# Semaphore clears of the first block's programs moved into the next program, those of the last stages merged

## The chip, the cores and the metric

The kernel runs on one core of a Trainium2 chip. The metric is the device time of one execution in microseconds (us). The engines are PE (TensorE, matmuls; PEld is its weight load), DVE (VectorE), ACT (ScalarE), POOL (GpSimd) and SP (SyncE, which here only issues DMAs). Each engine runs its own instruction stream; the streams meet through semaphores. A small letter q behind an engine's name in a row (PEldq, POOLq) marks an instruction of its sequencer, such as a semaphore clear, a drain or a wait.

## The reference

Two transformer blocks over 256 tokens of width 1024, in float32, one after the other:

```
x = first_block(...)     # modulated norm, then attention + long convolution + Fourier mixing, gated;
                         # then x + g2 * expert_choice_moe(h2, router, w_gate, w_up, w_down), 16 experts
return second_block(x, ...)   # two layers, each: x + 0.5*g1*swiglu(h); three mixers; x + 0.5*g3*swiglu(h)
```

The arithmetic, the tiles and the transfers are the same in both kernels. Only the housekeeping between programs differs, so nothing more of the reference is needed.

## The kernel before

The kernel is a row of hand-written programs. A program is one `nc.Block()`: in it every engine has its own list of instructions, and at its end all five engines meet in a barrier (a drain on each engine, then a semaphore event that POOL collects and gives back). A program belongs to a `Stage` (L268). A stage owns on-chip buffers (`sb`) and semaphores (`sem`), and both are given back when the `with` statement of the stage is left.

The semaphores must be zero again before they are used anew or before the kernel runs again. So `Stage.__exit__` (L298) opens a second `Block` after the program, a clean-up: every fifth semaphore is cleared by POOL (L303), the next by SP (L308), then by PE (L313), ACT (L318) and DVE (L323), all five engines side by side, and then they meet in that block's own barrier. In the profile the clean-up's barrier has line L299. Nothing else runs in a clean-up, and the next program can't start before it is over.

The stages nest. In order of time, with the line that the barrier of the stage's program has in the profile:

- `whole` holds 11 semaphores that show when a feed-forward panel has landed (`ff_here`), and encloses everything.
- `first` (L2771) holds 8 semaphores of the expert panels and encloses the first block. In it:
  - `mixer` (L2778) holds 16 semaphores, and encloses four programs: `front` (its program's barrier is L2606), `project_in` (L650), `attention` (L380) and `project_out` (L975).
  - a stage named `moe` (L2799) with buffers alone and no semaphore, around the program `moe` (L1184).
- `trunk` (L3495) holds 4 semaphores and encloses the second block: `first_layer` (L3525), `between` (L3555) and `last` (L3589).

Every stage with semaphores has one clean-up, so there are 12: after `front`, `project_in`, `attention`, `project_out`, `mixer`, `moe` and `first` in the first block, and after `first_layer`, `between`, `last`, `trunk` and `whole` in the second. Where two stages end together, as `project_out` and `mixer` do, their clean-ups follow each other with nothing between them.

`first_layer` and `between` already clear most of their semaphores inside their own programs: `clear_early` (L288) has POOL clear them (L291) while the other engines finish the layer. These two stages keep this in both kernels.

What sets the order of the work around the clean-ups:

- `project_in` starts with matmuls on panels that `front` loaded (L755).
- `attention` starts with DMAs for the next program's weights (L384) and with score matmuls (L392).
- `project_out` issues the first six expert panels of 2 MB (L1003) as its buffers come free.
- `moe` starts with routing: transposes on PE (L1265), then a chain on DVE. Its SP loads three more panels at once (L1188, L1190), and then one more for each panel that PE has consumed (L1193, waiting for `panel_done`). Its 16 experts have 12 panels each.
- `first_layer` starts with DVE and ACT making the normalized input, then matmuls on panels that landed during `moe` (L1629).
- POOL has no program in `project_in`, `attention`, `project_out`, `moe` and `last`: it only waits in their barriers.

Of the kernel before, what the change touches and what calls it, by code (L numbers as in the profile page):

```python
# [267 lines left out]
class Stage:  # L268


    count = 0

    def __init__(self, nc, name):
        Stage.count += 1
        self.nc, self.name = nc, f"{name}_{Stage.count}"

    def __enter__(self):
        self.stack, self.sems = ExitStack(), []
        return self

    def sb(self, name, shape, dt=F32):
        return self.stack.enter_context(self.nc.sbuf_tensor(f"{self.name}_{name}", shape, dt))[:]

    def sem(self, name):
        self.sems.append(self.stack.enter_context(self.nc.semaphore(f"{self.name}_{name}")))
        return self.sems[-1]

    def clear_early(self, pool, keep):  # L288
# [2 lines left out]
                pool.sem_clear(s)  # L291
        self.sems = list(keep)

    def block(self):
        return self.nc.Block()

    def __exit__(self, kind, value, trace):
        if kind is None and self.sems:  # L298
            with self.nc.Block() as block:  # L299
                @block.gpsimd  # L300
                def _(pool):
                    for s in self.sems[0::5]:
                        pool.sem_clear(s)  # L303

                @block.sync
                def _(sp):
                    for s in self.sems[1::5]:
                        sp.sem_clear(s)  # L308

                @block.tensor  # L310
                def _(pe):
                    for s in self.sems[2::5]:
                        pe.sem_clear(s)  # L313

                @block.scalar
                def _(sc):
                    for s in self.sems[3::5]:
                        sc.sem_clear(s)  # L318

                @block.vector  # L320
                def _(ve):
                    for s in self.sems[4::5]:
                        ve.sem_clear(s)  # L323
        self.stack.close()


# [19 lines left out]
class Chain:  # L346


    def __init__(self, eng, sem):
        self.eng, self.sem, self.n = eng, sem, 0  # L350
# [7 lines left out]
def attention(nc, c, ps, ar, q_of, k_of, v_of, out_of, n_pairs, n_keys, early):  # L358
# [2 lines left out]

    kt = n_keys // P
    n_prob = 6
    with Stage(nc, "attention") as st:
        prob = ar.take(n_prob, n_keys)
        probT = ar.take(4, kt, T)
        low = st.sb("low", [P, n_prob])
# [10 lines left out]
        mix_bank = lambda p: ps[6 + p % 2]  # L378

        with st.block() as block:  # L380
            @block.sync
            def _(sp):
                for slot, src, sem in early:
                    sp.dma_start(slot, src).then_inc(sem, 16)  # L384
# [215 lines left out]
def project_in(nc, c, ps, ring, extra, I, cst, tables, xT, hT, vec, cond, mod, gain, proj, kv, spare, in_slots, in_loaded,  # L600
# [1 line left out]

    with Stage(nc, "project_in") as st:
        h = hT[:, :, 0:T]
        buffers = [extra[:, at * T:(at + n) * T].rearrange("p (a b) -> p a b", b=T) for at, n in ((0, 4), (4, 1), (5, 1), (6, 2))]
        d = Dense(st, c, ring, ps, xT, h, "in", buffers, in_loaded)
# [39 lines left out]
        none = [0] * SLOTS  # L648
        pairs = proj.rearrange("p (q a) t -> p q (a t)", a=2)
        with st.block() as block:  # L650
            @block.sync
            def _(sp):
                def mod_panel(n):
                    if n >= len(side):

                        sp.wait_ge(mod_done, n - len(side) + 1)
                    sp.dma_start(side[n % len(side)], I["w_mod"][4 * first + n]).then_inc(mod_here[n % len(side)], 16)

                for n in range(len(side)):
                    mod_panel(n)  # L660
                rotary.sync(sp)
                for p in range(slots, turns * slots):

# [286 lines left out]
def project_out(nc, c, ps, I, ring, extra, early, late, xT, h, mod, gain, proj, mix, router, expert_slots, expert_loaded,  # L950
# [1 line left out]

    with Stage(nc, "project_out") as st:
        buffers = [extra[:, at * T:(at + n) * T].rearrange("p (a b) -> p a b", b=T) for at, n in ((0, 4), (4, 1), (5, 1), (6, 3))]
        d = Dense(st, c, ring, ps, xT, h, "out", buffers)
        spare = Arena(ring[:, 8 * BLK * P:], RING_COLS - 8 * BLK * P)
# [14 lines left out]
        sum_behind, turn_behind = {1: 0, 6: 1}, {2: 0, 7: 1}  # L973
        branch, out = (early + late)[:panels], (early + late)[panels:]
        with st.block() as block:  # L975
            @block.sync
            def _(sp):
                for slot, src, sem in late:
                    sp.dma_start(slot, src).then_inc(sem, 16)
                def side_panel(n):  # L980
                    if n >= len(side):

                        sp.wait_ge(side_done, n - len(side) + 1)
                    sp.dma_start(side[n % len(side)], fours(I["w_ada"][0, n])).then_inc(side_here[n % len(side)], 16)

                for n in range(len(side)):
                    side_panel(n)
                sp.dma_start(router, I["small1"][:, SM1["router"][0]:SM1["router"][1]]).then_inc(router_here, 16)
                sp.dma_start(t["vec"], I["vec2"][0]).then_inc(vec2_here, 16)

                for u in range(6):
                    if u == 1:
                        for n in range(len(side), len(side) + panels - 1):
                            side_panel(n)

                        sp.wait_ge(d.panel_done, panels)
                    if u == 3:
                        for n in range(len(side) + panels - 1, 8):
                            side_panel(n)
                    if u >= 3:  # L1000
# [136 lines left out]
def moe(nc, c, ps, cst, hT, place_of, x_sel, slot, slot_loaded, src, xT, gate, pool, w_ff, ff_here, x_gain):  # L1137
# [8 lines left out]
    up_panels, down_panels = KD, 4  # L1146
    slots, n = len(slot), KD + 4
    head = 4
    with Stage(nc, "moe") as st:
        e1 = st.sb("e1", [P, NT, E])  # L1150
        top = st.sb("top", [P, NT])
        tot = st.sb("tot", [P, NT])
# [29 lines left out]
        xs = x_sel.rearrange("p k (e s) -> p k e s", s=CAP)  # L1182
        quarter = [slice(g * CAP, (g + 1) * CAP) for g in range(4)]
        with st.block() as block:  # L1184
            @block.sync
            def _(sp):
                sp.dma_start(numbers, cst["slots"]).then_inc(numbers_here, 16)
                sp.dma_start(lead_slot, src[0, 0]).then_inc(lead_here, 16)  # L1188
                for u in range(6, slots):
                    sp.dma_start(slot[u], src[0, u + 1]).then_inc(slot_loaded[u], 16)  # L1190
                for r in range(slots + 1, 2 * n):
                    sp.wait_ge(panel_done, r - slots + 1)
                    sp.dma_start(slot[(r - 1) % slots], src[r // n, r % n]).then_inc(slot_loaded[(r - 1) % slots], 16)  # L1193
                sp.dma_start(ff_slot(pool, 0), w_ff[0]).then_inc(ff_here[0], 16)
                with sp.Fori(1, E // 2) as i:
                    for r in range(2 * n):

# [261 lines left out]
def ff_slot(pool, u):  # L1459
    return pool[:, KD * T + u * BLK * P:KD * T + (u + 1) * BLK * P]  # L1460
# [1118 lines left out]
def front(nc, c, ps, ring, extra, I, cst, vec, cond, xT, ctxT, hT, mod, gain, spec, slots, loaded, consts, consts_here):  # L2579
# [8 lines left out]
    n_panels, per_tile, width, tiles = 8, KD // 2, 2 * P, 2  # L2588
    rows = hT.rearrange("p k n -> p (k n)").rearrange("p (g t d) -> p g t d", g=2, t=NT)
    streams = ((xT, hT[:, :, 0:T]), (ctxT, hT[:, :, T:2 * T]))  # L2590
    with Stage(nc, "front") as st:
        spectrum = Spectrum(st, c, ps, cst, I["small1"][:, 0:SM1["router"][0]], vec, spec)
        sums = st.sb("sums", [P, width])
        sq, root, rstd = (extra[:, at * T:(at + n) * T].rearrange("p (a b) -> p a b", b=T) for at, n in ((0, 4), (4, 2), (6, 2)))
# [171 lines left out]
def first_block(nc, c, ps, pool, I, cst, vec, cond, xT, tables, t, ff_here):  # L2766
# [4 lines left out]
    with Stage(nc, "first") as st:  # L2771
# [3 lines left out]

        expert_slots = [ring[:, u * 4 * D:(u + 1) * 4 * D] for u in (5, 0, 1, 2, 3, 4)]
        expert_loaded = [st.sem(f"expert_loaded{u}") for u in range(8)]
        with Stage(nc, "mixer") as mx:  # L2778
            spec = mx.sb("spec", [P, 5, 512])
            ctxT = mx.sb("ctxT", [P, KD, T])  # L2780
            consts = ring[:, CONSTS_AT:CONSTS_AT + pack_cols("branch_consts")]
# [17 lines left out]
        with Stage(nc, "moe") as s2:  # L2799
# [685 lines left out]
def dense_buffers(st):  # L3485
    return [st.sb(k, [P, n, T]) for k, n in (("sq", 4), ("root", 1), ("rstd", 1), ("silu", 3))]


def second_block(nc, c, ps, pool, I, cst, vec1, cond, xT, tables, t, ff_here, out):
# [5 lines left out]
    with Stage(nc, "trunk") as tr:  # L3495
# [54 lines left out]
        with Stage(nc, "between") as st:  # L3550
# [4 lines left out]
            with st.block() as block:  # L3555
# [25 lines left out]
                def _(pool):  # L3581
                    enter.gpsimd(pool)
                    mixed.gpsimd(pool)
        with Stage(nc, "last") as st:
# [77 lines left out]
```

## Time and profile before

| | us |
|---|---|
| time, median of 3 runs | 2680.59 (2679.92 to 2684.70) |
| time of the profiled execution | 2676.57 |
| its span, first to last instruction | 2674.8 |
| PE busy in it | 2274.5 (85%) |
| DVE busy | 821.4 (31%) |
| ACT busy | 393.6 (15%) |
| POOL busy | 6.1 (0%) |
| mean rate of the DMAs | 270 GB/s, near 428 GB/s in `moe` |

PE's granted clock was 0.928 of full speed in the mean. The 12 clean-ups don't show as busy time: semaphore instructions aren't counted, so a clean-up looks like a short stretch in which all engines are idle. The rows that show them are asked for by their source line.

### The profile page before, as it was taken

How to read it: one execution, taken by the hardware profiler on the slowest of the kernel's cores; microseconds unless marked ns; L12 is line 12 of the kernel's file. 1: busy time of each engine (PE TensorE's matmuls, PEld its weight loads, DVE VectorE, ACT ScalarE, POOL GpSimd, SP SyncE). 2: the span in 40 equal slices, each digit the busy share in tenths (PEclk: the TensorE clock that was granted, in tenths of full speed). 3: DMA queues.
4: the chain of work that ended last, by engine and by line, in shares of the span. 5: the costliest groups of instructions: out<-in, count | busy, mean ns of one | idle time of the engine just before them, and what ended most of it. 6: DMA issues, size and time to landing. Idle time of an engine off the chain costs nothing. (4 is left out here: it accounts for less than half of the span.)

```text
span 2674.8 us, 29322 instructions
## 1 busy us (share of the span) xinstructions
PE 2274.5 (85%) x12064; PEld 1571.5 (59%) x12064; DVE 821.4 (31%) x1566; ACT 393.6 (15%) x859; POOL 6.1 (0%) x11
## 2 busy tenths in 40 slices
PE   8999876656556666666899999999999999999998
PEld 4786732111111111111788886888888888678887
DVE  4753631000010000000543267531034415753001
ACT  2203110000000000000200145210010004441000
POOL 0000000000000000000000000000000000000000
PEclk9999988887888778877999999999999999999999
DMA  9643789999999999999986321096458833106430
GB/s 374 234 173 151 292 354 427 427 428 428 428 427 428 428 429 428 428 428 425 387 307 223 128 92 64 19 367 246 147 214 308 305 133 111 71 2 252 147 121 16
DMA packets 74908, 721.62 MB, mean 270 GB/s; under 512 B 8624, under 2 KB 11696, under 8 KB 13232
## 3 DMA queue, kind: packets, MB, share of 16 engines
q1 hardware_dynamic: 74800, 720.09, 66.5%
q8 instruction: 79, 1.29, 0.2%
q14 instruction: 29, 0.24, 0.0%
HBM read 719.01 MB, written 1.05 MB: 269 GB/s over the span
## 5 line engine op out<-in xcount | busy, mean ns | idle before, releaser
L1629 PE MATMUL bank<-pool 128*128 128x256 f32 x2720 | 595.1, 380 | 6.2 <-ACT pool L1556 6.2
L1629 PEld LDWEIGHTS bank<-pool 128*128 128x128 f32 x2720 | 515.7, 190 | 81.6 <-issue 12.3
L1220 PE MATMUL bank<-pool,moe_x_cur 128*32 128x512 f32 x1792 | 272.5, 743 | 154.9 <-DMA pool<-in_w_expert 154.9
L1661 PE MATMUL bank<-trunk_proj,pool 128*128 128x256 f32 x1408 | 306.4, 379 | 0.0
L1661 PEld LDWEIGHTS bank<-trunk_proj,pool 128*128 128x128 f32 x1408 | 266.6, 190 | 36.6 <-issue 0.8
L1220 PEld LDWEIGHTS bank<-pool,moe_x_cur 128*32 128x32 f32 x1792 | 55.3, 123 | 357.7 <-DMA pool<-in_w_expert 251.7
L1235 PE MATMUL bank<-pool,moe_hidT 128*32 128x512 f32 x896 | 149.5, 801 | 89.2 <-DMA pool<-in_w_expert 85.7
L1387 DVE TENSOR_TENSOR moe_hid<-bank,moe_silu 128x512 f32<-128x512 f32 x16 | 11.1, 692 | 448.7 <-ACT moe_silu L1343 448.7
L1848 PE MATMUL bank<-pool 128*128 128x256 f32 x672 | 148.1, 380 | 0.0
L1235 PEld LDWEIGHTS bank<-pool,moe_hidT 128*32 128x32 f32 x896 | 28.7, 130 | 199.3 <-DMA pool<-in_w_expert 139.5
L1848 PEld LDWEIGHTS bank<-pool 128*128 128x128 f32 x672 | 127.3, 190 | 19.9 <-issue 2.6
L755 PE MATMUL bank<-pool 128*128 128x256 f32 x576 | 126.8, 379 | 2.3 <-PEq L299 2.3
L755 PEld LDWEIGHTS bank<-pool 128*128 128x128 f32 x576 | 109.2, 190 | 20.4 <-issue 6.0
L1249 PE MATMUL bank<-moe_place,moe_y 128*128 (+1 forms) x256 | 72.1, 431 | 43.8 <-DVE xT L1397 26.3
L1249 PEld LDWEIGHTS bank<-moe_place,moe_y 128*128 128x128 f32 x256 | 51.5, 211 | 78.3 <-DVE xT L1397 33.4
L1391 DVE COPY moe_y<-bank 128x512 f32<-128x512 f32 x16 | 11.1, 691 | 271.8 <-PE bank L1235 271.8
L1343 ACT ACTIVATE moe_silu<-bank 128x512 f32<-128x512 f32 x16 | 9.6, 597 | 568.2 <-PE bank L1220 568.2
L1668 DVE SCALAR_TENSOR_TENSOR xT<-bank,gain,xT 128x256 f32<-128x256 f32 x32 | 15.5, 484 | 246.1 <-PE bank L1661 246.0
L2113 DVE SCALAR_TENSOR_TENSOR trunk_consts<-pool,cond,trunk_consts 128x1024 f32<-128x1024 f32 x64 | 82.2, 1285 | 2.3
L1640 DVE TENSOR_TENSOR trunk_proj<-bank,between_silu 128x256 f32<-128x256 f32 x42 | 17.8, 424 | 196.8 <-ACT between_silu L1636 196.8
L1397 DVE SCALAR_TENSOR_TENSOR xT<-bank,first_mod,xT 128x256 f32<-128x256 f32 x128 | 53.1, 478 | 77.2 <-PE bank L1249 77.2
L2111 DVE SCALAR_TENSOR_TENSOR trunk_consts<-pool,cond,trunk_consts 128x1024 f32<-128x1024 f32 x48 | 61.4, 1279 | 1.9
(588 smaller groups left out, 2123.2 us busy)
## 6 DMA issues: line engine op xcount, KB each, us to landing
pool<-in_w_expert SPq DMA_DIRECT2D x168, 2048.0 KB, 35.7
pool<-in_w_ff SPq DMA_DIRECT2D x132, 1024.0 KB, 6.7
pool<-in_w_ada SPq DMA_DIRECT2D x66, 1024.0 KB, 5.8
moe_more<-in_w_expert SPq DMA_DIRECT2D x23, 2048.0 KB, 34.0
pool<-in_w_in SPq DMA_DIRECT2D x40, 1024.0 KB, 4.9
pool<-in_w_mod SPq DMA_DIRECT2D x24, 1024.0 KB, 7.4
pool<-in_w_out SPq DMA_DIRECT2D x10, 1024.0 KB, 10.5
pool<-in_small SPq DMA_DIRECT2D x2, 2560.0 KB, 13.4
```

The costliest lines, as they stand in the source:

```text
L755: mm = pe.matmul(ps[p % 3][:, j * T:(j + 1) * T], w[:, j * KD + k], h[:, k], start=k == 0, stop=k == KD - 1)
L1220: mm = pe.matmul(ps[b][quarter[g], :], x_cur[:, u], w[:, b, g], start=u == 0, stop=u == up_panels - 1)
L1235: mm = pe.matmul(ps[2 + b][quarter[g], :], hidT[:, s, g], w[:, g, b], start=s == 0, stop=s == down_panels - 1)
L1249: mm = pe.matmul(ps[at][:, (j % 2) * T:(j % 2 + 1) * T], y[:, k * P:(k + 1) * P], place_of[:, e], start=True, stop=True)
L1397: m = ve.scalar_tensor_tensor(xT[:, k], ps[at][:, (j % 2) * T:(j % 2 + 1) * T], gate[:, k:k + 1], xT[:, k], MUL, ADD)
L1629: mm = pe.matmul(self.ps[p % 3][:, j * T:(j + 1) * T], w[:, j * KD + k], self.hT[:, k], start=k == 0, stop=k == KD - 1)
L1640: ve.tensor_tensor(hid[:, p], self.ps[p % 3][:, T:2 * T], self.silu[:, p % 3], MUL).then_inc(self.bank_free, 1)
L1661: mm = pe.matmul(self.ps[3 + q % 2][:, 0:T], w, x[:, k], start=k == 0, stop=k == nk - 1)
L1668: ve.scalar_tensor_tensor(self.xT[:, q], self.ps[3 + q % 2][:, 0:T], gain[:, q:q + 1], self.xT[:, q], MUL, ADD).then_inc(self.x_updated, 1)
L1848: mm = pe.matmul(ps[n % 3][:, j * T:(j + 1) * T], slot[:, j * KD + k], hT[:, k], start=k == 0, stop=k == KD - 1)
L2111: ve.scalar_tensor_tensor(total, w[:, 0], cond[:, 2 * j, 2:3], total, MUL, ADD).then_inc(acc_step, 1)
L2113: ve.scalar_tensor_tensor(total, w[:, 1], cond[:, 2 * j + 1, 2:3], total, MUL, ADD).then_inc(side_done, 1)
```

## The change

A stage can be marked `late`. It then has no clean-up of its own: when it is left, its buffers are given back, but its semaphores stay taken and stand on a list, `Stage.late_ones`. Two things empty the list. Either the next program does it: `clear_late` has POOL clear all of them, one after the other, at the start of that program. Or the next stage that isn't late has one clean-up for its own semaphores and those on the list together.

```
+    late_ones = []
+    def __init__(self, nc, name, late=False):
...
+    def clear_late(self, pool):
+        for sems, held in Stage.late_ones:
+            for s in sems:
+                pool.sem_clear(s)
+            self.cleared.append(held)
+        Stage.late_ones = []
...
     def __exit__(self, kind, value, trace):
+        for held in self.cleared:
+            held.close()
+        if self.late:
+            Stage.late_ones.append((self.sems, self.held))
+        else:
+            sems = self.sems + [s for late, _ in Stage.late_ones for s in late]
+            if kind is None and sems:
+                with self.nc.Block() as block:
...                      # the five engines clear every fifth, as before
+            for _, held in Stage.late_ones:
+                held.close()
+            Stage.late_ones = []
+            self.held.close()
         self.stack.close()
```

Marked late: `attention`, `project_in`, `project_out`, both `moe` stages, `front`, `mixer`, `trunk` and `last`. Not late: `first`, `first_layer`, `between` and `whole`. In the programs of `project_in`, `attention`, `project_out` and `moe` stands now:

```
+            @block.gpsimd
+            def _(pool):
+                st.clear_late(pool)
```

So `project_in` clears `front`'s semaphores, `attention` those of `project_in`, `project_out` those of `attention`, and `moe` those of `project_out` and `mixer`. The semaphores of `moe` are cleared in the clean-up of `first`, those of `last` and `trunk` in that of `whole`. Of the 12 clean-ups 4 are left: after `first`, `first_layer`, `between` and `whole`.

## Rows read from the trace of the kernel before

**Rows 1.** The page: each engine's busy time, share of the span, instructions
```profile
PE 2274.5 (85%) x12064; PEld 1571.5 (59%) x12064; DVE 821.4 (31%) x1566; ACT 393.6 (15%) x859; POOL 6.1 (0%) x11
```

**Rows 2.** One line's instructions, L299: count, ns min/median/max, first and last start
```profile
L299 SPq EVENT_SEMAPHORE  x12: 17/17/17, 59.6 to 2674.7; - x12
```

**Rows 3.** The same view, clean-up after front: barrier before, barrier after
```profile
L2606 SPq EVENT_SEMAPHORE  x1: 17/17/17, 58.3 to 58.3; - x1
L299 SPq EVENT_SEMAPHORE  x1: 17/17/17, 59.6 to 59.6; - x1
```

**Rows 4.** The same view, clean-up after project_in, with PE's clears
```profile
L650 SPq EVENT_SEMAPHORE  x1: 17/17/17, 228.3 to 228.3; - x1
L313 PEldq EVENT_SEMAPHORE_RANGE_CLEAR  x11: 56/56/56, 228.5 to 229.7; - x11
L299 SPq EVENT_SEMAPHORE  x1: 17/17/17, 229.9 to 229.9; - x1
```

**Rows 5.** The same view, clean-up after attention
```profile
L380 SPq EVENT_SEMAPHORE  x1: 17/17/17, 258.8 to 258.8; - x1
L299 SPq EVENT_SEMAPHORE  x1: 17/17/17, 259.3 to 259.3; - x1
```

**Rows 6.** The same view, the two clean-ups after project_out, from 333.5 us
```profile
L975 SPq EVENT_SEMAPHORE  x1: 17/17/17, 333.5 to 333.5; - x1
L299 SPq EVENT_SEMAPHORE  x2: 17/17/17, 334.4 to 335.5; - x2
L299 POOLq EVENT_SEMAPHORE  x2: 17/17/17, 335.0 to 335.4; - x2
```

**Rows 7.** The same view, the two clean-ups after moe, from 1277.7 us
```profile
L1184 SPq EVENT_SEMAPHORE  x1: 17/17/17, 1277.7 to 1277.7; - x1
L313 PEldq EVENT_SEMAPHORE_RANGE_CLEAR  x7: 56/56/56, 1277.9 to 1278.6; - x7
L299 SPq EVENT_SEMAPHORE  x2: 17/17/17, 1278.9 to 1279.4; - x2
```

**Rows 8.** The same view, the three clean-ups at the end, from 2672.2 us
```profile
L3589 SPq EVENT_SEMAPHORE  x1: 17/17/17, 2672.2 to 2672.2; - x1
L299 DVEq DRAIN  x1: 128/128/128, 2673.9 to 2673.9; - x1
L299 SPq EVENT_SEMAPHORE  x3: 17/17/17, 2673.4 to 2674.7; - x3
```

**Rows 9.** Windows: start:end and length in us, busy us of PE, PEld, DVE, ACT, POOL, granted clock, DMA share, GB/s
```profile
332.00:336.00 4.00, 1.77 (x9) 1.69 (x9) 0.41 (x3) 0.45 (x1) 0.00 (x0) 0.50 0.07 27
340.00:344.00 4.00, 0.00 (x0) 0.00 (x0) 3.69 (x14) 0.00 (x0) 0.00 (x0) 0.78 0.99 422
348.00:352.00 4.00, 4.00 (x21) 4.00 (x20) 0.87 (x2) 0.28 (x1) 0.00 (x0) 0.50 0.96 410
356.00:360.00 4.00, 4.00 (x24) 1.46 (x22) 1.54 (x3) 0.39 (x1) 0.00 (x0) 1.00 0.00 0
360.00:364.00 4.00, 4.00 (x26) 1.25 (x28) 0.73 (x2) 0.00 (x0) 0.00 (x0) 1.00 1.04 348
400.00:1262.00 862.00, 535.80 (x3168) 146.46 (x3166) 71.14 (x151) 31.96 (x60) 0.00 (x0) 0.81 1.01 428
```

**Rows 10.** Timeline: start, us, engine, line, what; in brackets idle time before and its releaser
```profile
59.69 2.61 PE L755 MATMUL bank<-pool 128*128 128x256 f32 x11 [2.34 <-PEq L299]
335.59 3.49 PE L1265 MATMUL bank<-ident,pool 128*128 128x128 f32 x16 [2.23 <-PEq L299]
359.03 0.33 SPq L1193 DMA_DIRECT2D pool<-in_w_expert  x1
1280.02 0.17 DVE L2129 SCALAR_TENSOR_TENSOR gain<-mod,vec 128x8 f32<-128x8 f32 x1 [2.51 <-PEq L299]
```

**Rows 11.** One line's instructions and the timeline: POOL's clears beside PE's matmuls in first_layer
```profile
L291 POOLq EVENT_SEMAPHORE_RANGE_CLEAR  x119: 44/44/44, 1717.3 to 1726.0; - x119
1720.19 5.34 PE L3147 MATMUL bank<-trunk_mix,pool 128*128 128x256 f32 x24
```

More of the change, by code:

```diff
@@ L271 @@
     count = 0
-    def __init__(self, nc, name):
+    late_ones = []
+    def __init__(self, nc, name, late=False):
         Stage.count += 1
-        self.nc, self.name = nc, f"{name}_{Stage.count}"
+        self.nc, self.name, self.late = nc, f"{name}_{Stage.count}", late
     def __enter__(self):
-        self.stack, self.sems = ExitStack(), []
+        self.stack, self.held, self.sems, self.cleared = ExitStack(), ExitStack(), [], []
         return self
@@ L284, in sem @@
     def sem(self, name):
-        self.sems.append(self.stack.enter_context(self.nc.semaphore(f"{self.name}_{name}")))
+        self.sems.append(self.held.enter_context(self.nc.semaphore(f"{self.name}_{name}")))
         return self.sems[-1]
@@ L297, in __exit__, with _ @@
     def __exit__(self, kind, value, trace):
[L298 to L323, printed above, removed]
+        for held in self.cleared:
[8 more added lines that the diff above has]
+                    def _(pool):
+                        for s in sems[0::5]:
+                            pool.sem_clear(s)
+                    @block.sync
+                    def _(sp):
+                        for s in sems[1::5]:
+                            sp.sem_clear(s)
+                    @block.tensor
+                    def _(pe):
+                        for s in sems[2::5]:
+                            pe.sem_clear(s)
+                    @block.scalar
+                    def _(sc):
+                        for s in sems[3::5]:
+                            sc.sem_clear(s)
+                    @block.vector
+                    def _(ve):
+                        for s in sems[4::5]:
+                            ve.sem_clear(s)
+            for _, held in Stage.late_ones:
+                held.close()
+            Stage.late_ones = []
+            self.held.close()
         self.stack.close()
@@ L363, in attention @@
     n_prob = 6
-    with Stage(nc, "attention") as st:
+    with Stage(nc, "attention", late=True) as st:
         prob = ar.take(n_prob, n_keys)
@@ L380, in attention, with _ @@
         with st.block() as block:
+            @block.gpsimd
+            def _(pool):
+                st.clear_late(pool)
             @block.sync
@@ L601, in project_in @@
                consts_here, branch, spec):
-    with Stage(nc, "project_in") as st:
+    with Stage(nc, "project_in", late=True) as st:
         h = hT[:, :, 0:T]
@@ L650, in project_in, with _ @@
         with st.block() as block:
+            @block.gpsimd
+            def _(pool):
+                st.clear_late(pool)
             @block.sync
@@ L951, in project_out @@
                 final_g, t, cond, kv, spec, ctx_h):
-    with Stage(nc, "project_out") as st:
+    with Stage(nc, "project_out", late=True) as st:
         buffers = [extra[:, at * T:(at + n) * T].rearrange("p (a b) -> p a b", b=T) for at, n in ((0, 4), (4, 1), (5, 1), (6, 3))]
@@ L975, in project_out, with _ @@
         with st.block() as block:
+            @block.gpsimd
+            def _(pool):
+                st.clear_late(pool)
             @block.sync
@@ L1148, in moe @@
     head = 4
-    with Stage(nc, "moe") as st:
+    with Stage(nc, "moe", late=True) as st:
         e1 = st.sb("e1", [P, NT, E])
@@ L1184, in moe, with _ @@
         with st.block() as block:
+            @block.gpsimd
+            def _(pool):
+                st.clear_late(pool)
             @block.sync
@@ L2590, in front @@
     streams = ((xT, hT[:, :, 0:T]), (ctxT, hT[:, :, T:2 * T]))
-    with Stage(nc, "front") as st:
+    with Stage(nc, "front", late=True) as st:
         spectrum = Spectrum(st, c, ps, cst, I["small1"][:, 0:SM1["router"][0]], vec, spec)
@@ L2777, in first_block @@
         expert_loaded = [st.sem(f"expert_loaded{u}") for u in range(8)]
-        with Stage(nc, "mixer") as mx:
+        with Stage(nc, "mixer", late=True) as mx:
             spec = mx.sb("spec", [P, 5, 512])
@@ L2798, in first_block @@
                         expert_loaded, v("final_g"), t, cond, kv, spec, hT[:, :, T:2 * T])
-        with Stage(nc, "moe") as s2:
+        with Stage(nc, "moe", late=True) as s2:
             place = s2.sb("place", [P, E, T])
@@ L3494, in second_block @@
     small = ring[:, MIX_COLS:]
-    with Stage(nc, "trunk") as tr:
+    with Stage(nc, "trunk", late=True) as tr:
         proj = tr.sb("proj", [P, 24, T])
@@ L3583, in _ @@
                     mixed.gpsimd(pool)
-        with Stage(nc, "last") as st:
+        with Stage(nc, "last", late=True) as st:
             buffers = dense_buffers(st)
```

## The prediction

> **What bounds the kernel now.** I read the page first: PE is busy 85% of the span and POOL has hardly anything to do, 6.1 us [rows 1]. Nothing of the change touches PE's work, so the question is only what the idle stretches between programs cost. The page can't answer it, because semaphore instructions aren't counted as busy. So the second view is that of the clean-up's own line, L299: twelve releases of SP [rows 2], one for each stage with semaphores. The third is the same view cut to one clean-up at a time [rows 3 to 8]. In each the reader sees the release of the program's barrier (an event of SP) and that of the clean-up's barrier, in some PE's clears between them. The time between the two releases is time in which no engine works, and what comes behind it starts within 0.1 us (59.69 and 335.59 for PE) or, where DVE leads, after its waits (1280.02), each released through the barrier L299 [rows 10]. A clean-up is thus on the path of everything, whichever engine bounds the stages around it.
>
> **What a clean-up costs.** The barriers give 58.3 to 59.6 = 1.3 us after front [rows 3], 228.3 to 229.9 = 1.6 us after project_in [rows 4], 258.8 to 259.3 = 0.5 us after attention [rows 5], 333.5 to 335.5 = 2.0 us for project_out and mixer together [rows 6], 1277.7 to 1279.4 = 1.7 us for moe and first [rows 7] and 2672.2 to 2674.7 = 2.5 us for last, trunk and whole [rows 8]. Most of it follows the slowest clearer, PE: 11 clears from 228.5 to 229.7 are 0.12 us each [rows 4], and 7 from 1277.9 to 1278.6 the same [rows 7]. With 11 clears the clean-up took 1.6 us, so its fixed part is 1.6 - 11 x 0.12 = 0.3 us; 7 clears give 1.2 - 0.84 = 0.35. Not all are explained by this. In mixer's clean-up POOL's two events lie 0.4 us apart, at 335.0 and 335.4 [rows 6], and in trunk's a drain of DVE came only at 2673.9, half a microsecond after that clean-up began at 2673.4 [rows 8]. I call these two the pauses; each is worth about 0.3 us.
>
> **The change part by part.** *Five clean-ups go* (front, project_in, attention, project_out, mixer). Their barriers and clears leave the path: 1.3 + 1.6 + 0.5 + 2.0 = 5.4 us. The program's own barrier stays.
>
> *moe and first become one.* Together they hold 35 + 8 semaphores, PE clears every fifth, 9 of them: the 1278.9 - 1277.7 = 1.2 us of the clean-up with 7 clears [rows 7], plus 2 x 0.12, is 1.4 us in place of 1.7. Gain 0.3 us.
>
> *last, trunk and whole become one.* They hold 33 + 4 + 11 = 48, of which PE clears 10, where it cleared 7 for last alone: 2673.4 - 2672.2 = 1.2 us [rows 8], plus 3 x 0.12, is 1.5 to 1.6 us in place of 2.5. Gain 1.0 us, at the very end of the span, where nothing can take it back.
>
> *What is added:* POOL clears one after the other some 150 semaphores (42 of front, 56 of project_in, 9 of attention, 27 of project_out, 16 of mixer; PE's share of project_in's is a fifth, the 11 of [rows 4]). In first_layer POOL already does this beside work: 119 clears from 1717.3 to 1726.0, 0.073 us each [rows 11]. That makes about 3.1 us for front's 42 inside project_in, 4.2 for project_in's 56 inside attention, 0.7 inside project_out and 3.2 inside moe. What hides it is the program's length: 229.9 to 258.8 = 28.9 us for attention, the shortest [rows 4, 5]. POOL waits for nothing in these clears, nothing is queued behind them but its own drain for the barrier, and it would have to be 24 us late in attention to hold anyone. If that cover were gone, attention's barrier would come up to 4.2 us later. Do the clears slow the others' semaphore traffic? While they ran in first_layer, PE made 24 matmuls in 5.34 us, 0.22 us apart [rows 11], and with nothing beside them 11 took 2.61 us, no faster [rows 10]. I take nothing, with 0 as one end and, as the other, the case below where each clear holds up the path.
>
> *Does the gain reach the end?* Before moe it must pass a stage that waits for DMAs. From 400 to 1262 us the queue moves 428 GB/s with a share of 1.01 [rows 9], so moe ends when its stream of panels ends, and the stream could have started at a time that the clean-ups don't set. But between 356 and 360 us the DMA engines stand still (share 0.00) and from 360 on they run full [rows 9]: the nine panels ahead have landed and SP waits for PE to consume the first. The stream's start hangs on PE, PE on the routing, and the routing on the barrier at 335.5 [rows 10]. So the 5.4 us pass through. The same holds in front of project_in, whose panels have landed, and after moe, where DVE starts 0.6 us behind the barrier and PE waits for what DVE and ACT make [rows 10].
>
> *Sum:* 5.4 + 0.3 + 1.0 = 6.7 us. Against the profiled execution's own 2676.57 us this is 2669.9. That execution was 4.0 us faster than the median of the runs, 2680.59; I put the same gain on the median: 2680.59 - 6.7 = 2673.9 us.
>
> One rule of the notes bears on the pauses. The Trainium skill, "Runtime: NRT & Kernel Launch", section "Instruction fetch mechanics", says that instructions arrive in blocks of 16 KiB, that crossing into the next is mostly hidden, and that a taken branch to a target outside the window stalls the engine. The rows show a release at 228.3 followed by PE's first clear at 228.5 [rows 4], so that entering a clean-up costs no such stall; whether the two pauses are block crossings no row here shows. If they are, they would move and not vanish, and the sum would be 6.1 instead of 6.7 us.
>
> **The rivals.** *The two pauses come back elsewhere.* For it: they aren't explained by the number of clears. Removing instructions shifts all that follows on each engine. One or several pauses could then fall on a barrier that was smooth. Two back give 6.7 - 0.6 = 6.1 us, 2674.5; with three more, 0.9 us, 2675.4.
>
> *PE's clock at the start of moe.* The granted clock was 0.50 (1.2 GHz) from 332 to 336 us, where PE was busy only 1.77 of 4 us, was mixed in 340 to 344, where PE had nothing to do, 0.50 again in 348 to 352, and back at 1.00 (2.4 GHz) from 356 [rows 9]. The change takes 2.0 us of idle time out of just this stretch, and shifts it. A clock that stays low until 360 would double the 4.0 us of PE's work in 356 to 360 and perhaps as much ahead of it: 4 to 7 us lost, 2678 to 2681. A clock that comes back sooner could give up to 3 us, since PE's 1.77 us and the 4.00 in 348 to 352 would halve: 2670.9. Against both: PE's idle time while DVE picks the tokens (340 to 344) stays as it is. Beyond 361 the clock costs nothing here, because the panels come no faster. The Trainium skill, "TensorE: Matmul & The Clock Gate", Part 1, says the gate's window runs freely, so that one kernel differs from run to run; the spread of 4.8 us among the three runs would fit, but no row here ties it to the clock.
>
> *The DMA stream takes the gain.* If the stream in moe were set by something before 335 us, 5.4 us would be lost and 1.3 kept: 2679.3. The standstill at 356 to 360 [rows 9] speaks plainly against it.
>
> *The clears beside work hold others up (the slower side).* POOL's 150 clears go out at the head of four programs, where first waits, DMA landings and matmuls also use semaphores. If each held up the path by the 0.12 us that PE needs for one, this is 150 x 0.12 = 18 us against 6.7 gained: +11.3, 2691.9. It decides from 6.7 / 150 = 0.045 us a clear, and is slower by over 0.2% from (6.7 + 5.4) / 150 = 0.08 us. Against it: PE's even spacing during 119 such clears [rows 11].
>
> *The change doesn't do what it says:* if semaphores cleared late forced other waits, or the clean-ups stayed. The diff shows no added wait. I give it nothing beyond the other cases.
>
> **How the numbers follow.** Plain gain, 2673.9, own range 2671.5 to 2676.5 for the spread of medians: 0.62. Pauses come back, 2674.5 to 2675.4: 0.10. Clock worse, 2678 to 2681: 0.10; clock better, 2670.9: 0.08. Stream takes it: 0.06. Clears hold up: 0.04. The range 2670.0 to 2679.5 leaves out the clears and part of the bad clock. A measurement of this kernel can tell about 0.2%, 5.4 us, from no change, so the line is at 2675.2. The plain gain lies 1.3 us beyond it: with a scatter of a little over 1 us four fifths of it (0.50) are faster; with the better clock (0.08) and most of the pauses (0.06) this is 0.64. Slower by over 0.2% is only the clears, 0.04. Within 0.2%: 0.32.
>
> **What would show it.** L299 should have 4 releases in place of 12, with 43 and 48 clears in the merged ones, 1.4 and 1.5 us long. New POOL clears should stand at the head of four programs, 0.07 us apart, and POOL's drain should be over long before any barrier. From the barrier L650 to the first instruction of attention should be under 0.1 us instead of 1.7. The first reload of an expert panel should come 5.4 us earlier than at 359.03 [rows 10], and moe's stream should have the same length. I would be wrong if a program's length, start to barrier, grew by more than half a microsecond: in attention and project_in that would be the clears, at the start of moe the clock.

## The result and the profile after

The changed kernel takes 2668.34 us in the median of five executions (2666.26 to 2672.30), the kernel before 2680.71. The ratio is 0.9954, with a 95% interval of 0.9943 to 0.9965: 12.4 us faster, where 6.7 were forecast, and below the low end of the range, 2670.0. Two more comparisons gave 0.9959 (0.9945 to 0.9973) and 0.9944 (0.9930 to 0.9957). Over all comparisons, 120 executions of the kernel before have a mean of 2680.4 us, with a standard error of 0.2, and 15 of the changed kernel 2668.3 with 0.4. The gain is 12.1 us.

A single execution tells less than this. They scatter from 2672.6 to 2685.4 us before. The trace shown ahead of the prediction is of a quick one (2676.57), and the one of after is of the slowest of its five (2672.30), so that the two spans differ by only 4.3 us: the clean-ups give 7.0 us and front was 1.7 us shorter, but project_out was 1.6 and moe 2.7 us longer. What can be compared between two traces is a piece whose length repeats.

The page of after, its span and busy times (compare [rows 1]):

```profile
span 2670.5 us, 29234 instructions
PE 2282.2 (85%) x12064; PEld 1576.2 (59%) x12064; DVE 820.9 (31%) x1566; ACT 393.8 (15%) x859; POOL 6.1 (0%) x11
```

The clean-ups' barrier, now L314, and POOL's new clears (L299), by their line: count, ns min/median/max, first and last start. They answer [rows 2] and [rows 11]:

```profile
L314 SPq EVENT_SEMAPHORE  x4: 17/17/17, 1276.2 to 2670.5; - x4
L299 POOLq EVENT_SEMAPHORE_RANGE_CLEAR  x42: 44/44/48, 56.6 to 59.5; - x42
L299 POOLq EVENT_SEMAPHORE_RANGE_CLEAR  x56: 44/44/44, 225.3 to 229.6; - x56
L299 POOLq EVENT_SEMAPHORE_RANGE_CLEAR  x43: 44/44/44, 330.0 to 332.9; - x43
```

Four releases are left of twelve. POOL's clears follow each other at 0.07 us, 56 of them in 4.3 us, and end long before the barriers of their programs, which the same view shows as the answer to [rows 3 to 8]:

```profile
L2641 SPq EVENT_SEMAPHORE  x1: 17/17/17, 56.5 to 56.5; - x1
L673 SPq EVENT_SEMAPHORE  x1: 17/17/17, 225.3 to 225.3; - x1
L399 SPq EVENT_SEMAPHORE  x1: 17/17/17, 254.1 to 254.1; - x1
L1002 SPq EVENT_SEMAPHORE  x1: 17/17/17, 329.9 to 329.9; - x1
L1215 SPq EVENT_SEMAPHORE  x1: 17/17/17, 1274.8 to 1274.8; - x1
L3624 SPq EVENT_SEMAPHORE  x1: 17/17/17, 2668.9 to 2668.9; - x1
```

project_in lasts 225.3 - 56.5 = 168.8 us, as before (59.6 to 228.3, 168.7 by the rounded rows), and attention 254.1 - 225.3 = 28.8 (229.9 to 258.8). Neither pays anything for POOL's clears. The merged clean-ups last 1276.2 - 1274.8 = 1.4 and 2670.5 - 2668.9 = 1.6 us. All clean-ups together took 11.0 us in the trace before and take 4.1 in this one, so their own idle time accounts for 7.0 us (these sums are over the barriers' times to 0.01 us, finer than the rows print).

The timeline of PE after front, after project_in and after project_out, and SP's first reload of an expert panel (start, us, what, in brackets the idle time before it and what ended it; compare [rows 10]):

```profile
56.65 1.53 PE L782 MATMUL bank<-pool 128*128 128x256 f32 x6 [1.04 <-PEq L2641]
225.41 0.66 PE L415 MATMUL bank<-mixer_kv,mixer_proj 64*128 64x512 f32 x1 [0.72 <-PEq L673]
330.04 0.66 PE L1300 MATMUL bank<-ident,pool 128*128 128x128 f32 x2 [0.30 <-PEq L1002]
353.28 0.33 SPq L1228 DMA_DIRECT2D pool<-in_w_expert  x1
```

PE's idle time at the three boundaries is 1.0, 0.7 and 0.3 us. It was 2.3 at front and 2.2 at project_out [rows 10], and 2.3 at project_in by this line of the trace before:

```profile
230.06 0.66 PE L392 MATMUL bank<-mixer_kv,mixer_proj 64*128 64x512 f32 x1 [2.34 <-PEq L299]
```

The first reload of an expert panel comes at 353.28, 5.75 us earlier than at 359.03 [rows 10]. The 5.4 us that were forecast are in it; the rest is 0.2 us of a shorter head of moe and the 1.7 and 1.6 us by which front and project_out differ in these two traces.

In windows (columns as in [rows 9]), project_out's end and moe's start look like this:

```profile
322.00:326.00 4.00, 3.23 (x16) 3.26 (x16) 2.92 (x9) 3.49 (x9) 0.00 (x0) 0.52 1.00 430
330.00:334.00 4.00, 3.96 (x18) 3.54 (x18) 1.06 (x6) 3.73 (x9) 0.00 (x0) 0.50 0.70 193
342.00:346.00 4.00, 4.00 (x20) 4.00 (x20) 1.68 (x4) 0.28 (x1) 0.00 (x0) 0.50 1.01 434
346.00:350.00 4.00, 3.63 (x31) 2.01 (x30) 0.05 (x1) 2.37 (x3) 0.00 (x0) 0.99 0.21 88
```

The granted clock is about 0.50 (1.2 GHz) from project_out's end through the head of moe. It was so before too, but for part of the stretch from 340 to 344 us, where PE had nothing to do [rows 9]. So 7.0 us of the 12.1 are explained by what left the path, and 5.1 are not. The experiments are about these 5.1 us.

### The profile page after: what moved, and what is told of

Same layout as the page of the kernel before. It is cut to its first block and busy times, and to the rows that moved or that the text cites. A ratio compares the mean times of both kernels' runs of the same rounds, so it can differ in the third digit from the quotient of the medians.

```text
span 2670.5 us, 29234 instructions
## 1 busy us (share of the span) xinstructions
PE 2282.2 (85%) x12064; PEld 1576.2 (59%) x12064; DVE 820.9 (31%) x1566; ACT 393.8 (15%) x859; POOL 6.1 (0%) x11
## 5 line engine op out<-in xcount | busy, mean ns | idle before, releaser
L1284 PE MATMUL bank<-moe_place,moe_y 128*128 (+1 forms) x256 | 78.0, 458 | 43.7 <-DVE xT L1432 26.3
```

What stands on the lines that cost most here:

```text
L1284: mm = pe.matmul(ps[at][:, (j % 2) * T:(j % 2 + 1) * T], y[:, k * P:(k + 1) * P], place_of[:, e], start=True, stop=True)
```

## The experiments

Two things are read from each: the mean of its timed executions against the 2680.4 us of the kernel before, and the lengths of the stages in its trace, as the time from one barrier to the next. The second is one sample per kernel, but the 20 traces together show which lengths repeat and which take steps. The number in brackets behind a mean is its standard error in us. The theories A to D are stated in the expectations.

The 2680.4 us are pooled. Within single comparisons the kernel before had means from 2679.6 to 2681.5, so its level moves by somewhat more than the standard errors of 0.4 to 0.9 let expect, and a gain of 1 us in a single edit is not resolved. Where it matters, the gain against the executions of the same comparison is given as "own comparison"; the ratios are of that kind too. The changed kernel's three gains are 11.6 to 13.4 us counted so.

**Repeat the change, and take it apart.** The first kernel is the changed one. The second marks only `project_out` and `mixer` late, the third all but these two, the fourth only `trunk` and `last`; in each the other stages lose the mark, as here in the third:

```
-    with Stage(nc, "project_out", late=True) as st:
+    with Stage(nc, "project_out") as st:
...
-        with Stage(nc, "mixer", late=True) as mx:
+        with Stage(nc, "mixer") as mx:
```

> The changed kernel as it is, timed once more. Its clean-ups account for 6.7 us. Theory A (the clean-ups' idle time is all there is, the rest of the 12.4 us measured is scatter by the phase of PE's clock): the ratio's interval should reach up to 0.9975, that is a gain of 6.7 us, and its mean may lie anywhere from 5 to 12 us. Theory B (the shorter idle time also keeps PE's clock up somewhere, in every execution): again 11 to 13 us.

> Only the two clean-ups between project_out and moe go (2.0 us of idle time); their semaphores are cleared by POOL inside moe; all others stay. Theory A: 2.0 us faster, about 2678.7. Theory B, if the extra comes from PE's clock around the start of moe: 2.0 + 5.7 = 7.7 us faster, about 2673.

> The change without its part between project_out and moe: these two clean-ups stay. Theory A: 6.7 - 2.0 = 4.7 us faster, about 2676. Theory B with the start of moe as the place: the same 4.7 us. If the extra comes from another place, such as project_in or project_out: about 10.4 us faster, 2670.

> Only the last three clean-ups are merged into one, which can't change anything ahead of it. Both theories: 1.0 us faster, about 2679.7. What it differs from this by is the scatter of a comparison of five rounds, which is what the extra 5.7 us has to be weighed against.

Measured: the changed kernel 2668.1 in the mean, the gain is real. Dropping the pair before moe: 2675.8 (0.9), 4.6 us faster than the pooled before (own comparison 3.9; ratio 0.9984, 0.9975 to 0.9993). All but this pair: 2670.2 (0.9), 10.2 faster (own comparison 9.4; 0.9964, 0.9952 to 0.9976). The end alone: 2678.7 (1.0), 1.7 faster (0.9998, 0.9987 to 1.0008), which fits its 1.0. The third speaks for most of the excess lying elsewhere than before moe. Its trace and the fourth's gave the lead: project_in took 170.4 us in the fourth, whose clean-ups stay, and 168.8 in the third.

**One boundary at a time, longer idle time, and idle time filled.** The first two mark only `front` and only `project_in` late. The third is the kernel before with doubled clears at two places:

```
+        if kind is None and self.name.startswith(("front", "project_in")):
+            self.sems = self.sems * 2
```

The fourth is the kernel before, but in five clean-ups PE works instead of clearing:

```
                 def _(pe):
-                    for s in self.sems[2::5]:
-                        pe.sem_clear(s)
+                    if warm:
+                        ident, bank = Stage.busy
+                        for _ in range(max(1, len(self.sems[2::5]) // 3)):
+                            pe.matmul(bank[:, 0:2 * P], ident, Stage.wide, start=True, stop=True)
+                    else:
+                        for s in self.sems[2::5]:
+                            pe.sem_clear(s)
```

`warm` holds for front, project_in, attention, project_out and mixer. There SP makes PE's clears, and PE's matmuls go to a bank that nobody reads.

> Only front's clean-up goes (1.3 us); project_in's POOL clears its semaphores. Theory A (idle time of the clean-up only): 1.3 us faster. Theory C (PE's idle time of 2.3 us at each program boundary lets its clock fall to 1.2 GHz in some executions, as in the profile of the kernel with the merged end, where it was low for 3.4 us from 57.7 us and project_in took 1.6 us more; without the clean-up PE is idle for 1 us and the clock stays): 1.3 us plus up to 1.6 us, so 2 to 3 us faster on average.

> Only project_in's clean-up goes (1.6 us); attention's POOL clears its semaphores. Theory A: 1.6 us faster. Theory C: 1.6 us plus up to 1.6 us, so 2 to 3 us faster on average, and attention never longer than its 28.8 us.

> The kernel before, but after front and after project_in every semaphore is cleared twice, so these two clean-ups are about 1.0 and 1.3 us longer and PE idles 3.3 and 3.6 us there instead of 2.3. Theory A: 2.3 us slower, about 2682. Theory C: the clock falls at these two places in most executions: 2.3 us plus 1 to 3 us, so 3.5 to 5.5 us slower, and the trace shows the low clock right behind the boundary, with project_in at 170.4 us instead of 168.8.

> The kernel before with all its clean-ups, but in the five after front, project_in, attention, project_out and mixer SP makes PE's clears, and PE makes 2, 3, 1, 1 and 1 matmuls whose results nobody reads. The clean-ups last about as long as before (within 0.3 us each), yet PE is idle for less than 1 us at a time. Theory A: no change, within 1.5 us of before. Theory C: faster by the extra part, 3 to 5 us, though no clean-up was removed.

Measured: front alone 2678.0 (0.5), 2.4 us faster, of which 1.3 are the clean-up. project_in alone 2677.8 (0.8), 2.6 faster, of which 1.6. In their own comparison the two gained 1.6 and 1.8 us, hardly more than the clean-ups themselves. Doubled clears: 2680.3 (1.0), no slower beyond the error (own comparison 0.7 slower; ratio 1.0001, 0.9990 to 1.0011), though the clean-ups are 1.8 us longer in sum in its trace, 2.4 us at the two places. Theory A had said 2.3 us slower, which the interval (up to 2.9) still holds; theory C had said 3.5 to 5.5, which lies outside. Its trace does show theory C's mark, twice: the clock was low behind both boundaries, project_in took 170.5 us and attention 29.6. But project_out took 72.6 us where the traces so far had 74 or 76. In this one trace that gave the time back; whether it does so in the other ten executions is not shown.

PE busy in the clean-ups: 2677.4 (0.7), 3.1 us faster than the kernel before (own comparison 2.2; 0.9990, 0.9981 to 0.9999), though its clean-ups last 13.1 us in its trace instead of 11.0. At equal length that is 5.2 us (own comparison 4.3), with an error of about 0.8: close to the 5.1 us in question, with no clean-up removed. Its timeline after front, and the window over this boundary (each call of a matmul in float32 stands in the trace as two, so the two that were added are four):

```profile
56.70 1.10 PE L317 MATMUL bank<-xT,ident 128*128 128x256 f32 x4 [1.04 <-PEq L2613]
58.10 0.67 PE L762 MATMUL bank<-pool 128*128 128x256 f32 x2 [0.30 <-PEq L299]
56.00:60.00 4.00, 3.00 (x13) 2.40 (x14) 0.40 (x1) 0.00 (x0) 0.00 (x0) 1.00 0.45 129
```

PE never idles longer than 1.0 us at this boundary, and the program behind it begins at 2.4 GHz. This is the strongest result for an effect of PE's idle time.

**Smaller parts, and three together.** Only `attention` late; only the two `moe` stages late, so that moe's and first's clean-ups are one; `front`, `project_in` and `attention` late; the changed kernel again.

> Only attention's clean-up goes (0.5 us); project_out's POOL clears its semaphores. Theory A (idle time alone): 0.5 us faster. Theory C (clock at the boundaries): PE idles 1.3 us here with the clean-up and 0.8 without, too little either way, so again 0.5 us, within 1.5.

> Only the clean-ups of moe and first become one (0.3 us). Theory A: 0.3 us faster. Theory D (what is still unexplained of the gain sits at the end of moe, where PE idles 6.2 us and its clock is low in every trace): 0.3 us plus 2 to 4 us. Theory C: 0.3 us, within 1.5.

> The clean-ups of front, project_in and attention go together (3.4 us), everything else stays. Alone, front's and project_in's gave 1.6 and 1.8 us in the means. Theory A: 3.4 us faster. Theory C with the effects adding up: 3.4 us and 0.5 to 1.5 on top, 4 to 5. If the pieces don't add up but work together: 6 us or more, as the change without its part before moe gave 9.4 us in the means where 4.7 were its clean-ups.

> The changed kernel a third time, for its scatter and one more trace: 10 to 12.5 us faster by the two comparisons so far. In the stage lengths project_in should be 168.8 us and attention 28.8, never more, and what differs from the two traces so far should be front, project_out, the first and the last 25 us of moe and the head of first_layer, by steps that go with stretches of low clock.

Measured: 2678.9 (0.4), 2677.6 (0.3), 2675.4 (0.8) and 2668.1 (0.7). Against the pooled before these are 1.5, 2.8, 5.0 and 12.3 us, in their own comparison 2.7, 3.9, 6.1 and 13.4. Attention alone gave 1.0 us beyond its clean-up, the first three together 1.6 beyond their 3.4, which is no more than what front and project_in gave beyond theirs one by one (1.1 and 1.0). By the pooled mean this is theory C's forecast for the three, 4 to 5 us. The merge gave 2.5 us beyond its 0.35, which theory C had not said.

The trace of the first of these shows what a low clock at the head of a program costs. These are windows of it, two behind front's clean-up and two behind project_in's:

```profile
56.00:60.00 4.00, 1.69 (x6) 0.68 (x4) 0.69 (x1) 0.00 (x0) 0.00 (x0) 1.00 0.24 100
60.00:64.00 4.00, 4.00 (x13) 3.27 (x12) 0.00 (x0) 0.00 (x0) 0.00 (x0) 0.60 0.87 305
228.00:232.00 4.00, 1.63 (x9) 1.27 (x9) 0.33 (x2) 1.06 (x2) 0.00 (x0) 0.94 0.01 2
232.00:236.00 4.00, 3.99 (x11) 1.24 (x10) 2.06 (x4) 2.32 (x6) 0.00 (x0) 0.63 0.80 303
```

and the window 60 to 64 in the kernel before, whose project_in starts 0.2 us later, and in the changed kernel, where it starts 2.8 us earlier:

```profile
60.00:64.00 4.00, 4.00 (x20) 3.54 (x19) 0.00 (x0) 0.00 (x0) 0.00 (x0) 1.00 0.76 287
60.00:64.00 4.00, 4.00 (x20) 3.54 (x19) 2.04 (x2) 0.17 (x1) 0.00 (x0) 1.00 1.01 424
```

PE is busy all the time in all three, but with a granted clock of 0.60 it gets 13 matmuls done and with 1.00 twenty. The barriers around these programs, in the trace with the low clock:

```profile
L314 SPq EVENT_SEMAPHORE  x1: 17/17/17, 59.4 to 59.4; - x1
L673 SPq EVENT_SEMAPHORE  x1: 17/17/17, 229.8 to 229.8; - x1
L314 SPq EVENT_SEMAPHORE  x1: 17/17/17, 231.5 to 231.5; - x1
L399 SPq EVENT_SEMAPHORE  x1: 17/17/17, 261.6 to 261.6; - x1
```

project_in 170.4 us instead of 168.8, attention 30.1 instead of 28.8.

**Controls, and a faster version.** The kernel before against itself; the changed kernel with moe and first not merged; with front's clean-up kept; and the changed kernel with PE busy where it idles longest around the start of moe:

```
                 pe.wait_ge(router_here, 16)
+                for _ in range(14):
+                    pe.matmul(ps[2][:, 0:P], c["ident"], c["ones"], start=True, stop=True)
...
                 mm.then_inc(turned, 1)
+                for _ in range(12):
+                    pe.matmul(ps[7][:, 0:2 * P], c["ident"], xT[:, 0], start=True, stop=True)
                 pe.wait_ge(placed, 1)
```

> The kernel before against itself, unchanged, as the measure of what such a comparison can tell. All theories: ratio 1, within 1 us. If it came out 1.5 us or more faster than before, the excess of the single edits would be an artefact of the comparison.

> The changed kernel, but moe keeps its own clean-up, so that it and first aren't merged. Theory C (clock at the boundaries with 2.3 us of idle PE): 0.35 us slower than the changed kernel, about 11 us faster than before. Theory D (the end of moe carries 2 to 4 us of the extra): only 7 to 9 us faster than before.

> The changed kernel with front's clean-up left in. Theory A: 1.3 us slower than the changed kernel. Theory C: 1.3 us plus the 1.7 us of a low clock at the head of project_in in about two executions of three, together 2.4 us slower than the changed kernel, so about 9 us faster than before.

> The changed kernel, and PE makes matmuls that nobody reads where it idles longest around the start of moe: 14 of 128 columns behind the second turn in project_out, where it waits 3.5 us for the normalized input, and 12 of 256 columns in moe after the turned affinities, where it waits 6.3 us for the picked tokens. If the clock falls there because PE is idle, it stays at 2.4 GHz: the router's 32 matmuls take 3.5 us instead of 7.0, and project_out and the head of moe together get 4 to 7 us shorter, so 15 to 18 us faster than before. If not, the 12 matmuls run at the low clock, take 10 us instead of 5 and hold up the picks: 3 to 5 us slower than the changed kernel.

Measured: before against itself 0.9997 (0.9987 to 1.0007), mean 2680.0 (0.9), so the excess of the full change is no artefact of the comparison. Without the merge 2668.9 (0.6), only 0.6 us slower than the changed kernel (forecast 0.35 by theory C, 2 to 4 by theory D); theory D falls for the full change. With front's clean-up kept 2671.6 (1.0), 3.3 us slower than the changed kernel, where theory A said 1.3 and theory C 2.4; with errors of 1.0 and 0.4 this leans to C but doesn't rule out A. In its one trace the clock did not fall behind front.

The busy version: 2664.8 (0.9), ratio 0.9937 to before (0.9924 to 0.9951), 3.5 us faster than the changed kernel, with an error of 1.0, and 15.6 faster than before, where 15 to 18 were forecast. It is the fastest of all. Its timeline, PE alone, from project_out's end to the picks:

```profile
319.56 3.29 PE L1079 MATMUL bank<-ones,ident 128*128 128x128 f32 x28
323.12 3.75 PE L1083 MATMUL bank<-first_router,pool 128*128 128x16 f32 x32 [0.28 <-ACT pool L1595]
330.16 6.12 PE L1310 MATMUL bank<-xT,ident 128*128 128x256 f32 x24
337.84 3.81 PE L1320 MATMUL bank<-moe_place 128*128 128x128 f32 x32 [0.90 <-DVE moe_place L1467]
```

and the same places in the changed kernel:

```profile
322.77 6.98 PE L1081 MATMUL bank<-first_router,pool 128*128 128x16 f32 x32 [3.50 <-ACT pool L1591]
340.40 0.39 PE L1309 MATMUL bank<-ident,moe_y 16*128 16x16 f32 x2 [6.28 <-DVE moe_y L1457]
341.69 5.90 PE L1316 MATMUL bank<-moe_place 128*128 128x128 f32 x32 [0.90 <-DVE moe_place L1463]
```

The added matmuls fill most of the two waits (x28 and x24 are 14 and 12 calls), the router's 32 matmuls take 3.75 us instead of 6.98 and the 32 of the gather 3.81 instead of 5.90. The clock did fall once, at the start of moe, and was up again for most of the added matmuls there:

```profile
330.00:334.00 4.00, 4.00 (x17) 3.44 (x16) 3.39 (x11) 0.99 (x3) 0.00 (x0) 0.79 0.96 394
334.00:338.00 4.00, 2.73 (x14) 2.05 (x13) 3.41 (x11) 0.00 (x0) 0.00 (x0) 1.00 1.01 430
```

project_out lasts 71.2 us in this trace (74.2 to 75.8 in the three traces of the changed kernel), and the head of moe, from its start to the first reload, 20.3 (23.0 to 23.4 in the three). That is 6 us or more, of which the timing shows 3.5; where the rest goes was not looked into.

**The two loose ends.** The merge once more, and the kernel before with PE busy only in the two clean-ups before moe:

> Only the clean-ups of moe and first merged, a second time. If the first result (2677.6 in the mean, where 0.35 us is its share) was scatter: 0 to 1.5 us faster than before. If the merge brings something by itself that the full change hides: again 3 us or more.

> The kernel before, but in the two clean-ups between project_out and moe PE makes one matmul each and SP its clears. By the trace of the kernel with all five so changed, this pair then lasts 3.3 us instead of 1.9, and PE is idle there for 0.6 us at a time instead of 2.2. Theory A: 1.4 us slower than before. Theory C at this place, with the 1.9 us that dropping the pair brought beyond its own length: 0.5 us faster than before.

Measured: the merge 2678.4 (0.4), 2.0 us faster (own comparison 2.6), between its two forecasts. Both runs of it together give some 2 us beyond its own 0.35, while leaving it out of the full change costs 0.6. Busy before moe: 2681.5 (1.0), 1.1 us slower than before (own comparison 0.5) with clean-ups that are 1.4 longer. Theory A had said 1.4 slower and theory C 0.5 faster, so this is nearer to A, and filling PE's idle time at this place brings no gain that can be told from nothing. The five clean-ups with a busy PE gained 5.2 us at equal length. That would put most of it on the other three, front, project_in and attention, but the kernel without just these three clean-ups gained only 1.6 us beyond their length (own comparison 2.6). The two results don't fit together well, and which boundary brings what is not shown.

## Why the prediction was wrong

**What a clean-up costs:** right. 6.7 us were worked out, 7.0 went. 5.4 for the five, 0.35 for moe and first, 1.0 at the end as forecast; another 0.2 came from between's clean-up, which had a pause of its own and lost it, a thing the rival about moving pauses had allowed in the other direction only.

**POOL's clears are hidden:** right, by project_in and attention, whose lengths are the same within 0.01 us in the two traces. The rival that had them hold others up is out.

**The gain passes moe:** right. From the first reload to the landing of the last expert panel it is 904.6 us in the trace before, 905.0 after, and 904.4 to 905.0 in all 20. The stream starts when PE releases the first panel, and the standstill of the DMAs before it [rows 9] was the right thing to look for.

**The sum stands for the whole effect:** this step failed. It took a clean-up's price to be its own length and let the clock in only as a rival at moe's start, with more chance for a loss (0.10) than for a gain (0.08) and a gain of at most 3 us. The range therefore ended at 2670.0. What the runs show in its place is a gain 5.1 us larger than the clean-ups' length, 12.1 against 7.0. The kernel with a busy PE in unshortened clean-ups says that the missing term lies in the idle time that the clean-ups give PE: filling it was worth 4.3 to 5.2 us. Part of the term is seen directly. Where PE idled 2.3 us or more behind front (3.4 in the kernel with doubled clears), project_in took 170.4 us instead of 168.8 in 5 of 11 traces; where it idled 1.0 or less, in none of 9. Where it idled 2.3 or more behind project_in, attention was 0.7 to 1.3 us longer in 4 of 10, otherwise in none of 10. The head of moe was 23.8 us in the mean of 11 traces with 1.9 us or more of idle PE before it and 23.2 in 8 without (the version with added matmuls in moe not counted). In the mean this is 0.75 + 0.45 + 0.55 = 1.75 us.

The granted clock that is on record for every execution points the same way. Its mean is 0.9275 (0.0002) over 115 executions of the kernel before, 0.9303 (0.0006) over the 15 of the changed kernel, 0.9309 (0.0006) with PE busy in five clean-ups, but 0.9272 (0.0010) with PE busy only before moe and 0.9276 (0.0007) with front's clean-up alone dropped. So PE had the low clock less where the excess is large. It is no proof of the 5.1 us: in the traces most of the low clock, 300 to 351 us of 361 to 408, lies in the body of moe, whose stream of panels takes the same time all the same.

The rows for it were there: [rows 10] have PE idle 2.34 us at the head of project_in, and [rows 9] a clock that falls around idle stretches. But the trace before was of an execution in which the clock stayed up at this boundary, and one trace can't show what happens in others. I read the spread of 4.8 us among three runs as noise around the effect instead of as a second price that the idle stretches might set. The Trainium skill, "TensorE: Matmul & The Clock Gate", Part 1, cited ahead for a gate that runs freely so that one kernel differs from run to run, agrees with this: the same program start had the low clock in some traces and not in others. Its consequence was not drawn.

**What stays open:** 3.4 of the 12.1 us, the difference between the 8.7 that the traces place (7.0 + 1.75) and the whole. That they too come from PE's idle time is what the kernel with a busy PE in five clean-ups suggests; no stage length shows them. The single edits don't add up either: front, project_in and attention gave 1.1, 1.0 and 1.0 us beyond their own lengths, together 1.6; doubled clears cost nothing, which is the result that speaks most against a price for every microsecond of idle PE; dropping the pair before moe gave 2.6 us beyond its 2.0, though a busy PE there gave nothing clear; the merge gives 2 us alone and 0.6 in the full change. Stages that no edit touches take steps too: front's program ends between 56.5 and 60.7 us, project_out takes 74.2 or 75.9, moe's last part, from the last panel's landing, 12.5 to 16.6 us. The first two go with the granted clock: front lasts 55.8 to 56.8 us in the 12 traces without a low clock between 36 and 44 us of the span, 57.3 to 57.6 in 6 with a short low stretch there and 58.9 and 60.0 in the two where that stretch is twice as long; project_out takes 75.8 to 76.0 us in the 10 traces with a low stretch 51 us behind its start, and 71.2 to 74.3 in the 10 without. What makes the clock fall there in one execution and not in another, and whether dropping the clean-ups makes it rarer, was not shown; this is the rival that stays beside a price of each idle stretch at its own boundary.

## What to carry to other kernels

A barrier with housekeeping between two programs costs what it lasts and, where it leaves TensorE idle between two busy stretches, in some executions a slow start of what follows; put the housekeeping on an engine that has nothing to do, inside the next program. Price an idle stretch from several traces and many executions, since a single one can miss a cost that falls in half of them. Where an idle stretch can't go, filling it with matmuls that nobody reads can pay: it gave 3.5 us at two waits here, and nothing clear in the two clean-ups before moe.

## What the runs showed of the hardware

- POOL makes a semaphore clear every 0.07 us beside the work of the other engines, and 56 in a row cost attention nothing; PE needs 0.12 us for one.
- At the start of project_in the granted clock fell to 1.2 GHz behind an idle stretch of PE of 2.3 us (3.4 in one) in 5 of 11 traces, and never behind 1.0 us in 9. In a window with a granted clock of 0.60, PE made 13 matmuls where it made 20 at 1.00.
- With twelve added matmuls, 6.12 us of work in a wait of 6.3 us, the granted clock was 1.00 from 334 to 338 us, where it was 0.50 in the changed kernel's trace without them, and the 32 matmuls behind the wait took 3.81 us instead of 5.90.
- A stream of 183 expert panels that keeps the DMAs full took 904.4 to 905.0 us in 20 traces, a spread of 0.07%, while executions as a whole spread by 0.5%.
